# Mixing stage of a two-block transformer kernel: queries and keys of the stick-breaking heads turned by DMA as 16-bit planes instead of by TensorE

## The reference, cut to what matters

```
def hybrid_mixer(u, positions, w_in, b_gate, w_branch_moba, w_branch_sb, w_out):
    proj = u @ w_in
    ...
    q_a, k_a, v_a, q_b, k_b, v_b, g_a, g_b = jnp.split(proj, cuts, axis=-1)
    q_a = partial_rotary(split_heads(q_a, N_HEADS_MOBA), positions)
    k_a = partial_rotary(split_heads(k_a, N_HEADS_MOBA), positions)
    y_a = merge_heads(moba_attention(q_a, k_a, split_heads(v_a, N_HEADS_MOBA)))
    y_b = merge_heads(stick_breaking_attention(split_heads(q_b, N_HEADS_SB), ...))
    gates = jax.nn.sigmoid(jnp.concatenate([g_a, g_b], axis=-1) + b_gate)
    ...
    merged = gate_a * (y_a @ w_branch_moba) + gate_b * (y_b @ w_branch_sb)
    return merged @ w_out
```

## Time and profile before

| what | value |
|---|---|
| median of 3 runs | 1217.35 us (1217.04 to 1218.85) |
| the profiled execution: its time | 1218.67 us |
| the profiled execution: its span | 1216.9 us |
| PE busy | 1206.9 us, 99% of the span |
| PEld busy | 994.2 us, 82% |
| DVE busy | 776.3 us, 64% |
| ACT busy | 683.1 us, 56% |
| POOL busy | 74.2 us, 6% |
| granted clock of PE | 0.999 of full speed |
| HBM read | 219.78 MB, 181 GB/s over the span |

### The profile page before, as it was taken

The page is one execution under the profiler, slowest core; times in us unless marked ns, Lnnn a source line. Parts: engine busy times, 40 slices in busy tenths (PEclk is TensorE's granted clock), DMA queues, the critical chain, the costliest instruction groups (busy, mean ns, idle before and its releaser), DMA issues.

```text
span 1216.9 us, 17161 instructions
## 1 busy us (share of the span) xinstructions
PE 1206.9 (99%) x5689; PEld 994.2 (82%) x5689; DVE 776.3 (64%) x1088; ACT 683.1 (56%) x1003; POOL 74.2 (6%) x123
## 2 busy tenths in 40 slices
PE   8999999999999999999999999999999999999998
PEld 6888888877788888888888788888888887888887
DVE  5655556697866665557668666655556666655554
ACT  5655545575555655547566576655555447654543
POOL 2320000000000000000220110000000001000000
PEclk9999999999999999999999999999999999999999
DMA  9867764545456989765555427866655544776771
GB/s 306 240 202 220 236 197 132 182 153 156 141 179 207 239 242 242 236 160 162 171 165 180 153 67 239 249 201 201 207 172 158 172 156 143 210 223 204 221 224 43
DMA packets 204929, 230.96 MB, mean 190 GB/s; under 512 B 51728, under 2 KB 146064, under 8 KB 204880
## 3 DMA queue, kind: packets, MB, share of 16 engines
q1 hardware_dynamic: 164784, 214.81, 56.9%
q10 hardware_dynamic: 38304, 9.76, 4.4%
q0 software_dynamic: 1792, 5.75, 1.9%
HBM read 219.78 MB, written 1.05 MB: 181 GB/s over the span
## 4 chain that ended last, share of the span: by engine, by line
PE 95%; ACT 1%; DVE 1%; DMA 1%; POOL 1%; issue 0%; SPq 0%; POOLq 0%
PE bank L1915 30%; PE bank L1917 29%; PE bank L1916 29%; PE bank L1971 2%; PE bank L2148 1%; PE bank L2164 1%; PE bank L2135 1%; DMA sb_gates<-h_xT 0%; PE bank L2133 0%; ACT sb_probs L1186 0%; DMA sb_raw<-e_w_in 0%; ACT sb_wh L716 0%; POOL sb_gates L602 0%; PE bank L2010 0%; PE bank L2473 0%
## 5 line engine op out<-in xcount | busy, mean ns | idle before, releaser
L1915 PE MATMUL bank<-sb_wh,sb_aTh 128*128 128x512 f32 (+1 forms) x1132 | 440.8, 389 | 1.7 <-DVE sb_wl L1267 1.7
L1917 PE MATMUL bank<-sb_wh,sb_aTl 128*128 128x512 f32 (+1 forms) x1132 | 435.1, 384 | 0.0
L1916 PE MATMUL bank<-sb_wl,sb_aTh 128*128 128x512 f32 (+1 forms) x1132 | 434.9, 384 | 0.0
L1267 DVE TENSOR_TENSOR sb_wl<-sb_raw,sb_wh 128x1024 fp32r<-128x1024 f32 x271 | 327.5, 1221 | 97.2 <-ACT sb_wh L716 92.7
L716 ACT ACTIVATE sb_wh<-sb_raw 128x1024 fp32r<-128x1024 f32 (+1 forms) x273 | 285.7, 1054 | 113.5 <-PE bank L1917 41.2
L1915 PEld LDWEIGHTS bank<-sb_wh,sb_aTh 128*128 128x128 f32 x1132 | 213.2, 188 | 44.0 <-issue 3.5
L1917 PEld LDWEIGHTS bank<-sb_wh,sb_aTl 128*128 128x128 f32 x1132 | 213.2, 188 | 42.6
L1916 PEld LDWEIGHTS bank<-sb_wl,sb_aTh 128*128 128x128 f32 x1132 | 213.4, 189 | 40.1
L1267 DVE TENSOR_TENSOR sb_wl<-sb_z,sb_wh 128x1024 fp32r<-128x1024 f32 x132 | 160.3, 1233 | 37.1 <-ACT sb_wh L716 37.1
L716 ACT ACTIVATE sb_wh<-sb_z 128x1024 fp32r<-128x1024 f32 x132 | 137.2, 1057 | 63.2 <-PE bank L1917 46.4
L1915 PE MATMUL bank<-sb_wh,sb_hTh 128*128 128x512 f32 x320 | 125.0, 391 | 0.0
(11 more groups left out here) (223 smaller groups left out, 910.8 us busy)
## 6 DMA issues: line engine op xcount, KB each, us to landing
sb_raw<-w_in SPq DMA_DIRECT2D x80, 256.0 KB, 3.0
sb_z<-ffn_w_down SPq DMA_DIRECT2D x64, 256.0 KB, 4.4
sb_z<-w_down SPq DMA_DIRECT2D x64, 256.0 KB, 3.8
sb_raw<-w_gate SPq DMA_DIRECT2D x54, 256.0 KB, 3.4
sb_raw<-w_up SPq DMA_DIRECT2D x54, 256.0 KB, 4.1
sb_raw<-ffn_w_gate SPq DMA_DIRECT2D x53, 256.0 KB, 3.6
sb_raw<-ffn_w_up SPq DMA_DIRECT2D x53, 256.0 KB, 4.3
sb_raw<-e_w_in SPq DMA_DIRECT2D x40, 256.0 KB, 3.0
```

What stands on the lines that cost most here:

```text
L1267: dve.tensor_tensor(wl[:, u % NSPLIT, :], raws[SLOT[u]], wh[:, u % NSPLIT, :].bitcast(F32), ALU.subtract).then_inc(low_done, 1)
L1915: pe.matmul(dst, lh, w_hi, start=start, stop=False)
L1916: pe.matmul(dst, lh, w_lo, start=False, stop=False)
L1917: return pe.matmul(dst, ll, w_hi, start=False, stop=stop)
```

## The change

The eight transposes of q_b and the eight of k_b are taken off PE. Instead ACT copies the low 16-bit halves of the chunk into a plane and DVE the high ones, each 128 x 1024 elements; ACT issues one DMA transpose over both planes (128 x 2048 elements of 16 bits, 16 blocks of 128 x 128), and ACT and DVE each join one plane into `qkT`. The planes lie in `junk`, the turned planes in the last two buffers of `probs`. For q_b the planes are made at ACT's and DVE's step 4 and joined at their step 8; for k_b they are made at step 8, right behind that join, and joined at step 13. ACT issues the DMA behind its split of that step. PE waits for both joins of k_b ahead of its first scores, after unit 13. The factor 0.125 moves into DVE's addition of the mask, which becomes a scalar_tensor_tensor for all heads. The evacuations of q_a and k_a are numbered anew.

```diff
+        qk_planes = junk[:, :].bitcast(U16)
+        qk_planesT = probs[:, 2:4, :].rearrange("p a c -> p (a c)").bitcast(U16)
...
+        def qk_plane(m, h):
+            halves = z[:, :, m, :].bitcast(U16).rearrange("p t (c h) -> p h t c", h=2)
+            return qk_planes.rearrange("p (h t c) -> p h t c", h=2, t=NT)[:, h], halves[:, h]
+
+        def qk_join(m, h):
+            halves = qkT[:, m, :, :].rearrange("p k t -> p (k t)").bitcast(U16).rearrange("p (k t r h) -> p h k t r", k=4, t=NT, h=2)
+            return halves[:, h], qk_planesT.rearrange("p (h t k r) -> p h k t r", h=2, t=NT, k=4)[:, h]
...
 ACT:
+            def qk_turn(m, u):
+                act.wait_ge(mix_evac_a, m + 1)
+                act.wait_ge(mix_evac_d, m + 1)
+                copy(*qk_plane(m, 0)).then_inc(qk_planed[0], 1)
+                act.wait_ge(qk_planed[0], m + 1)
+                act.wait_ge(qk_planed[1], m + 1)
+                split(u)
+                act.dma_start_transpose(qk_planesT.rearrange("p (b r) -> p b r", r=P), qk_planes).then_inc(qk_turned, 16)
+
+            def qk_joins(m):
+                act.wait_ge(qk_turned, 16 * m + 16)
+                copy(*qk_join(m, 0)).then_inc(qk_joined[0], 1)
...
             for v in range(4, 44):
-                if v == 6:
-                    qt_evac(mix_at, 0, 0.125)
-                if v == 10:
-                    qt_evac(mix_at, 1, 1.0)
...
-                split(u0 + v)
+                if v in (8, 13):
+                    qk_joins(0 if v == 8 else 1)
+                if v in (4, 8):
+                    qk_turn(v // 4 - 1, u0 + v)
+                else:
+                    split(u0 + v)
...
 DVE:
+            def qk_split(m):
+                dve.wait_ge(mix_evac_a, m + 1)
+                dve.wait_ge(mix_evac_d, m + 1)
+                dve.tensor_copy(*qk_plane(m, 1)).then_inc(qk_planed[1], 1)
+
+            def qk_joins(m):
+                dve.wait_ge(qk_turned, 16 * m + 16)
+                dve.tensor_copy(*qk_join(m, 1)).then_inc(qk_joined[1], 1)
...
-                ins = dve.tensor_tensor(s, bank[4 + i % 2][:, 0:384], bias[:, :], ALU.add)
+                scale = 0.125 if kind == "sb" else 1.0
+                ins = dve.scalar_tensor_tensor(s, bank[4 + i % 2][:, 0:384], scale, bias[:, :], ALU.mult, ALU.add)
...
-                if v == 6:
-                    qt_evac(mix_at, 0, 0.125)
-                if v == 10:
-                    qt_evac(mix_at, 1, 1.0)
+                if v in (8, 13):
+                    qk_joins(0 if v == 8 else 1)
+                if v in (4, 8):
+                    qk_split(v // 4 - 1)
...
 PE:
             def mix_steps(v):
+                if v == MIX_SCORES[0]:
+                    pe.wait_ge(qk_joined[0], 2)
+                    pe.wait_ge(qk_joined[1], 2)
...
-                if v == 6:
-                    qt(mix_at, 0, 0, lambda: evacuated(1))
-                if v == 10:
-                    qt(mix_at, 1, 1, lambda: evacuated(2))
                 if v == 13:
                     evacuated(3)
-                    pe.wait_ge(mix_at.qt_evac_a, 2)
-                    pe.wait_ge(mix_at.qt_evac_d, 2)
```

More of the change, by code:

```diff
@@ L324, in two_block_kernel @@
         wf_low = sem("wf_low")
+        qk_planed = [sem("qk_planed_a"), sem("qk_planed_d")]
+        qk_turned = sem("qk_turned")
+        qk_joined = [sem("qk_joined_a"), sem("qk_joined_d")]
         pool_chain = sem("pool_chain")
@@ L901, in qt_evac @@
             def qt_evac(at, k, scale):
-                act.wait_ge(at.qt_psum, 2 * k + 1)
+                act.wait_ge(at.qt_psum, 2 * (k - 2) + 1)
                 copy(qkT[:, k, 0:2, :], bank[QT_BANKS[k]][:, :], scale).then_inc(at.qt_evac_a, 1)
+            def qk_turn(m, u):
[9 more added lines that the diff above has]
+                copy(*qk_join(m, 0)).then_inc(qk_joined[0], 1)
             def mix_high(m):
@@ L1431, in qt_evac @@
             def qt_evac(at, k, scale):
-                dve.wait_ge(at.qt_psum, 2 * k + 2)
+                dve.wait_ge(at.qt_psum, 2 * (k - 2) + 2)
                 dve.tensor_scalar(qkT[:, k, 2:4, :], bank[QT_BANKS[k] + 1][:, :].rearrange("p (h t) -> p h t", h=2), scale, None, ALU.mult)\
                    .then_inc(at.qt_evac_d, 1)
+            def qk_split(m):
[5 more added lines that the diff above has]
+                dve.tensor_copy(*qk_join(m, 1)).then_inc(qk_joined[1], 1)
             def rotate(m):
@@ L2104, in qt @@
                 ready()
-                if k >= 1:
-                    pe.wait_ge(at.qt_evac_a, k)
-                    pe.wait_ge(at.qt_evac_d, k)
+                if k >= 3:
+                    pe.wait_ge(at.qt_evac_a, k - 2)
+                    pe.wait_ge(at.qt_evac_d, k - 2)
                 for g in range(2):
@@ L2208, in _ @@
                 if v == 25:
-                    pe.wait_ge(mix_at.qt_evac_a, 4)
-                    pe.wait_ge(mix_at.qt_evac_d, 4)
+                    pe.wait_ge(mix_at.qt_evac_a, 2)
+                    pe.wait_ge(mix_at.qt_evac_d, 2)
                 if v < 40:
```

## The result

The changed kernel takes 1220.15 us (median of 13 runs, 1219.26 to 1222.64) against 1217.35 us: a ratio of 1.0026, 95% interval 1.0019 to 1.0034 (the ratios are estimated from all executions, so they are not exactly the quotients of the medians). It is slower by 2.8 us and lies above the forecast's range (1215.0 to 1219.8). One of the 13 executions of the kernel before that ran beside it took 2186.65 us and is not counted; the others lie between 1216.52 and 1219.07. Its profiled execution took 1219.9 us, with a span of 1218.1.

What follows compares the result with a forecast made beforehand. PE, busy 99% of the span, was taken to bound the kernel. 1.95 us off PE less a 1.3 us wait at the first scores leaves 0.65: 1217.35 - 0.65 = 1216.7 us, range 1215.0 to 1219.8.

Steps and rivals of the forecast that it cites:

- gain on PE: Both turnings on PE: removing the 16 transposes saves 1.06 and 0.89 us, together 1.95 us, the most possible.
- price of the multiply-add: DVE's mask step in 24 heads: the multiply-add was taken to cost 0 more than the addition.
- copies: Two plane copies and two joins on each engine: 1.0 us apiece on ACT, 0.8 us on DVE.
- transfers: Each 16-block DMA transpose was taken to land 7 us after issue, bounded by 4.1 and 20.6 us.
- Rival C: Transfers are long and end last, deciding from about 10 us; at 12 us 1221.2, at 20.6 us 1238.5; chance 0.12.
- The way to the first scores: Queues followed from q_b's half to k_b's join at 234.4: scores at 234.5, PE waiting 1.3 us.
- I take 3.6: Loads of units 11 and 15: a unit's two loads take 3.6 us from first issue to last landing.
- Rival B: Each of the two loads in the chain takes 4.4 us instead of 3.6; scores 0.9 us later, 1218.3; chance 0.18.
- forecast stall of 1.3 us: PE waits 1.3 us ahead of the first scores for DVE's join of k_b, queued behind unit 16's low part.
- After the scores all queues run as before: Past the first scores: queues unchanged, only earlier, as PE sets the pace there too; no loss.
- sign of being wrong in kind: Low part late for PE between 212 and 235 us, or time appearing after the first scores, in the heads' steps.
- Rival A: All hidden on the way to the scores: join at 233.0, before PE's 233.2; full 1.95 us gained, 1215.4; chance 0.25.

Runs made afterwards that it cites:

- e9: Kernel before with only the multiply-add in place of the addition of the scores' two parts; 1217.6 us, ratio 1.0002 to the kernel before.
- e3: Changed kernel without the two DMA transposes and the waits for them, joins copying zeros; 1217.37 us, ratio 0.9999 to the kernel before.
- e2: Changed kernel with PE's wait for v_b's halves moved from before unit 13 to behind it; 1220.52 us, ratio 1.0031 to the kernel before.
- e1: Changed kernel with 11 filler matmuls on zeros ahead of PE's wait before unit 13; 1219.04 us, ratio 1.0017 to the kernel before.
- e10: Kernel before without the 16 PE transposes of q_b and k_b and nothing in their place; 1216.34 us, ratio 0.9993 to the kernel before.
- e11: e6 with PE's waits for v_b's halves and k_a's evacuation moved behind units 13 and 25; 1215.96 us, ratio 0.9988 to the kernel before.
- e5: Changed kernel with both engines' halves of v_b taken ahead of unit 15's split; 1219.2 us, ratio 1.0014 to the kernel before.
- e6: e5 with the join of k_b at step 12 instead of 13; 1217.17 us, ratio 1.0000 to the kernel before.
- e4: Changed kernel with ACT's split ahead of the plane, both joins one step earlier, DVE's v_b half ahead of unit 15's low part; 1223.76 us, ratio 1.0052.
- e7: e6 with ACT's split ahead of the plane copy at steps 4 and 8; 1218.98 us, ratio 1.0014 to the kernel before.

## Why the prediction was wrong

**The gain on PE was right.** 1.95 us forecast, 1.98 in the ledger. So was the price of the multiply-add (e9), of the copies (0.69 to 0.76 us on DVE where I took 0.8, 1.06 for ACT's plane where I took 1.0, though 1.36 for its join), and the transfers: 4.7 and 6.5 us against 7. Rival C (whose far end adds up to 1238.4, not 1238.5) decides from 10 us and is out; nobody waited for a transfer itself in the changed kernel.

**"The way to the first scores" failed in its last third.** Its times against the trace, to which 1.6 us are added, since the profiled execution of before ran that much later:

| step | forecast | measured + 1.6 |
|---|---|---|
| low part of unit 8 done | 214.6 | 214.9 |
| low part of unit 11 done | 220.4 | 220.9 |
| plane of k_b done | 222.7 | 222.8 |
| low part of unit 12 done | 224.9 | 225.2 |
| unit 15 landed | 228.5 | 229.9 |
| DVE's half of v_b done | not in the working | 232.9 |
| join of k_b done | 234.4 | 235.8 |
| first scores | 234.5 | 237.5 |

- Up to the low part of unit 12 it holds within 0.5 us.
- **"I take 3.6"** for a unit's two loads is the term that was mis-sized: unit 15 took 4.6, from 223.66 to 228.25, beside the second transfer. With the 0.3 us of the steps ahead this is 1.3 us. Rival B had just this, but for both loads; unit 11's took 3.7. e3, without the transfers, has unit 15's split 3.4 us after unit 12's low part (224.5 to 227.9), the changed kernel 4.7 (223.6 to 228.3).
- **PE's wait for v_b's halves was overlooked.** I followed the queues to the join and did not ask who else on PE waits for what is in them. By my own numbers DVE's half of v_b would have ended at 231.4, and PE, ready for unit 13 at 230.4, would have stood 1.0 us there. That alone would have cost nothing more, as e2 shows: it takes the place of the wait at the scores.
- **The clock had no term at all.** The forecast stall of 1.3 us came out as 2.6, and 1.7 us came on top of it. e1, with PE kept busy, has none of that.
- **"After the scores all queues run as before"** was wrong by 0.8 us, ahead of unit 25; time after the first scores was also my own sign of being wrong in kind. I read only the idle time of PE there, which is none, and took a busy PE for one with slack behind it. e10 shows 0.7 us of it without transfers, copies or joins. What it keeps of the change is a PE queue shorter by 16 transposes; the queues of ACT and DVE keep pace with PE, and unit 22's load, issued in time, takes 1.2 us longer in e10 and 1.3 in the changed kernel, with the instruction packet beside it.

The sum: -0.65 forecast, 1.3 more of waiting, 1.7 of clock and 0.8 at unit 25 make +3.15, and -0.34 elsewhere gives +2.8.

**Rival A** (all hidden, 1215.4 us) is what e11 reached, at 1216.0, but only with the edits of e5, e6 and e11 on top of the change.

**Settled:** the gain on PE is real and can be kept. e6 takes away the waits on the way to the scores, e10 shows the rest of the loss without any DMA transpose, and e11 takes that away too. **Open:** whether the instruction packet alone makes unit 22's load longer. Its place fits all 14 traces, but no run moved it alone, and no load was changed. Also e11's interval comes within 0.03% of no change; its ledger says 1.9 us, its median 1.5.

## What to carry to other kernels

When work moves off the engine that bounds, list every wait of that engine on the engines that take the work over, with its slack in the trace of before, over the whole stretch in which their queues run late, and not only the wait that the change adds. Place each such wait where the data is read, and put the result that PE needs next ahead of work that it needs four units later. A stall of some microseconds has a second price, the clock behind it, and a short one may have none. And when instructions leave a busy engine's queue, its instruction packets fall elsewhere in its work: look at which loads they fall into, and how much slack the waits behind these loads have.

## What the runs showed of the hardware

**A DMA transpose keeps the loads waiting.** The DMA view of the changed kernel over one microsecond, 224.5 to 225.5, with the queue of the transposes (q10) and no row for that of the loads (q1), though both loads of unit 15 had been issued by 224.4:

```profile
DMA packets 1010, 0.26 MB, mean 259 GB/s; under 512 B 1010, under 2 KB 1010, under 8 KB 1010
## 3 DMA queue, kind: packets, MB, share of 16 engines
q10 hardware_dynamic: 1010, 0.26, 124.9%
```

A load with no transpose beside it moves its first packet 0.95 to 0.98 us after its issue (unit 22 before, unit 15 in e3); unit 15's in the changed kernel came after 2.09 us, and the two loads took 4.6 us instead of e3's 3.4.

The Trainium skill (DMA: Bandwidth & Descriptors, "Issuing engines are not separate DMA queues") says that DMAs of all engines run on the same 16 engines and interleave, and that the time to start one is usually small beside the DMA. The trace agrees on the sharing; in this microsecond nothing interleaved, and the issue held ACT's queue for 1.7 to 3.4 us of a transfer of 4.6 to 8.4.

The Trainium skill (Advanced Engine Details and Errata, "X-Bar Transpose (TRN2)") expects 350 to 400 GB/s of a transpose. Here it moved 259 GB/s in this microsecond, where it had the engines to itself, and 207 GB/s from 213.3 to 214.5, where the first transfer did.

**The time to issue 16 blocks is not a constant.** 2.32 and 3.09 us in the changed kernel, 1.72 and 1.84 in e4, 3.43 and 1.71 in e7, against 1.25 to 1.41 for 8 blocks. What sets it is open.

**An instruction packet lengthens a load.** Unit 22's two loads took 3.3 and 3.4 us with the 16-KB packet of the instruction queue ahead of them (before, e9), 3.7 to 5.1 with it beside them (eleven kernels), and 3.3 with it behind them (e2). The packet comes at the same count of PE's matmuls in every kernel, within 4 of 1080.

**The clock after a still stand.** It fell to half behind stalls of 2.4 us (the changed kernel, e2) and 3.9 us (e4), and not behind those of 1.8 us (e5), 1.5 (e7) and 0.9 (e1), each in one execution. Over all executions the mean granted clock is below 1.000 in 23 of 25 of the changed kernel, e2 and e4, in 9 of 22 of e5 and e7, in 1 of 11 of e1, and in 21 of 89 of the kernel before, which has no such stall. The stretch near the beginning, in the profiled executions of before, e3, e4 and e9 and in none of the other ten, shows that the same stall can go either way. PE's timeline of the kernel before ahead of it, where PE waits for POOL and then has eight matmuls of 8 columns:

```profile
20.86 1.06 PE L1998 MATMUL bank<-sb_ones,sb_gates 128*128 128x8 f32 x8 [0.95 <-POOL sb_gates L603]
...
22.91 0.63 PE L1916 MATMUL bank<-sb_wl,sb_aTh 128*128 128x512 f32 x1
```

In the changed kernel the wait is 0.92 us and in e1 0.95 as here, and in both the clock holds. It costs 1.6 us where it falls, more than the forecast difference of the two kernels: two profiled executions are not to be compared end to end without looking for it.
